# An fp32r transformer block on one Trainium2 core: activation tiles moved to other places of 512 bytes

## What is computed

```python
# first block: mixer, then gated FFN
y = sigmoid(ga) * ((hm * gain * sigmoid(om)) @ w_mlstm_down) + sigmoid(gb) * y_b
mix = y @ w_mix_out
f = (gelu(causal_dwconv(gate)) * val) @ w_ffn_down      # val, gate = split(h @ w_ffn_up)
# second block: attention and conformer convolution, cross attention, MLP
xq = rmsnorm(h, norm_x_g) @ w_xq
mn = rmsnorm(mem, norm_mem_g);  xk = mn @ w_xk;  xv = mn @ w_xv
h = h + xo @ w_xo
h = h + square(relu(rmsnorm(h, norm_mlp_g) @ w_up)) @ w_down
```

## Time and profile before

| | us |
|---|---|
| median of 2 runs | 1605.63 |
| the runs | 1605.50, 1605.77 |
| span of the profiled execution | 1604.7 |
| TensorE busy in the span | 1574.8 |
| weight loads | 1289.5 |
| VectorE busy | 753.8 |
| ScalarE busy | 637.3 |
| GpSimd busy | 680.4 |

### The profile page before, as it was taken

One profiled execution on the slowest core, in us unless ns is written; L12 is line 12 of the kernel. 1 busy time (PEld: TensorE's weight loads), 2 busy tenths in 40 slices (PEclk: granted clock), 3 DMA queues, 4 the chain that ended last, 5 costly groups with the idle time before them and its releaser, 6 DMA issues.

```text
span 1604.7 us, 19156 instructions
## 1 busy us (share of the span) xinstructions
PE 1574.8 (98%) x7560; PEld 1289.5 (80%) x7560; DVE 753.8 (47%) x1333; ACT 637.3 (40%) x1145; POOL 680.4 (42%) x518
## 2 busy tenths in 40 slices
PE   7999999999997999999999999999999999999998
PEld 5788867788896888888888887778878888888886
DVE  5999424646586352133308799752442421012203
ACT  3543563453434332233322335672452442224322
POOL 1584233244543544444455464004314444444442
PEclk8999999999999999999999999999999999999999
DMA  9576522278533353333333432002212332333332
GB/s 316 131 114 148 132 79 79 65 224 289 196 92 118 107 171 124 98 101 92 97 123 102 137 105 89 5 14 79 80 39 84 102 103 99 99 93 92 105 94 78
DMA packets 221706, 180.31 MB, mean 112 GB/s; under 512 B 24232, under 2 KB 184360, under 8 KB 221488
## 3 DMA queue, kind: packets, MB, share of 16 engines
q1 hardware_dynamic: 214512, 167.00, 35.8%
q10 hardware_dynamic: 7104, 12.08, 2.2%
HBM read 172.49 MB, written 6.55 MB: 112 GB/s over the span
## 4 chain that ended last, share of the span: by engine, by line
PE 76%; DVE 4%; ACT 2%; POOL 0%; issue 0%; DMA 0%; DVEq 0%; ACTq 0%
PE bank L631 13%; PE bank L632 13%; PE bank L637 13%; PE bank L714 9%; PE bank L713 9%; PE bank L718 9%; PE bank L758 2%; PE bank L1105 1%; PE bank L1076 1%; PE bank L741 1%; PE bank L742 1%; PE bank L743 1%; PE bank L1162 1%; PE bank L967 1%; PE bank L1148 0%; PE bank L1149 0%
## 5 line engine op out<-in xcount | busy, mean ns | idle before, releaser
L2455 POOL TENSOR_TENSOR w_lo<-raw,w_hi 128x512 fp32r<-128x512 f32 (+1 forms) x484 | 646.6, 1360 | 871.6 <-ACT w_hi L1232 871.0
L1232 ACT ACTIVATE w_hi<-raw 128x512 fp32r<-128x512 f32 (+1 forms) x484 | 276.2, 620 | 336.5 <-PE bank L718 255.9
L631 PE MATMUL bank<-h_hi,w_hi 128*128 128x512 f32 x936 | 367.2, 392 | 0.0
L632 PE MATMUL bank<-h_lo,w_hi 128*128 128x512 f32 x936 | 364.3, 389 | 0.0
L637 PE MATMUL bank<-h_hi,w_lo 128*128 128x512 f32 x936 | 250.3, 389 | 0.0
L631 PEld LDWEIGHTS bank<-h_hi,w_hi 128*128 128x128 f32 x936 | 175.7, 188 | 39.0 <-issue 2.4
L632 PEld LDWEIGHTS bank<-h_lo,w_hi 128*128 128x128 f32 x936 | 175.7, 188 | 36.6 <-issue 0.7
L637 PEld LDWEIGHTS bank<-h_hi,w_lo 128*128 128x128 f32 x936 | 175.7, 188 | 36.6
L2282 DVE SCALAR_TENSOR_TENSOR bank<-att_area,cols,bank 128x512 f32<-128x512 f32 x116 | 87.6, 755 | 3.9
L713 PE MATMUL bank<-w_hi,u_hi 128*128 128x512 f32 x224 | 87.1, 389 | 0.0
L714 PE MATMUL bank<-w_hi,u_lo 128*128 128x512 f32 x224 | 87.1, 389 | 0.0
(11 more groups left out here) (439 smaller groups left out, 2639.9 us busy)
## 6 DMA issues: line engine op xcount, KB each, us to landing
raw<-in_w_in SPq DMA_DIRECT2D x57, 512.0 KB, 4.2
raw<-in_w_ffn_up SPq DMA_DIRECT2D x44, 512.0 KB, 3.9
raw<-in_w_up SPq DMA_DIRECT2D x32, 512.0 KB, 4.0
raw<-in_w_down SPq DMA_DIRECT2D x32, 512.0 KB, 3.7
ada_ring<-in_w_ada SPq DMA_DIRECT2D x24, 512.0 KB, 5.8
raw<-in_w_ffn_down SPq DMA_DIRECT2D x20, 512.0 KB, 3.7
raw<-in_w_s_glu SPq DMA_DIRECT2D x16, 256.0 KB, 3.1
raw<-in_w_mlstm_down SPq DMA_DIRECT2D x8, 512.0 KB, 6.7
```

The source lines that it names most:

```text
L631: te.matmul(ps, wv[0][:, i, :], rh, start=(i == 0), stop=False)
L632: te.matmul(ps, wv[0][:, i, :], rl, start=False, stop=False)
L1232: sc.activation(W_HI[SLOT[key]][:, part_], raw[:, RAW_SLOT[key], part_], ACT.Copy).then_inc(*hi_set.up((key, n_)))
L2455: gp_.tensor_tensor(W_LO[s_][:, part_], raw[:, RAW_SLOT[key], part_], W_HI[s_][:, part_].bitcast(F32), ALU.subtract).then_inc(*lo_made.up( ...
```

## The change

Only places of tiles in SBUF. The assertion asks for even elements instead of multiples of 128. No instruction is added, removed or reordered.

```diff
--- before.py
+++ after.py
@@ -186,7 +186,7 @@
             for s_ in shape:
                 n *= s_
             assert BASE + 4 * (at + n) <= END, name
-            assert dt == F32 or at % P == 0, name
+            assert dt == F32 or at % 2 == 0, name
             return nc.alloc_sbuf_tensor_at(name, [P, *shape], dt, offset=BASE + 4 * at)
 
         NRAW, NSPL, BW, NSCR = 3, 3, 1024, 3
@@ -267,7 +267,7 @@
         y_hi = place("y_hi", X + 8192, [KD, S], F32R)
         y_lo = place("y_lo", X + 12288, [KD, S], F32R)
         g_hi = place("g_hi", X + 4096, [KD, S], F32R)
-        g_lo = place("g_lo", X + 23680, [KD, S], F32R)
+        g_lo = place("g_lo", X + 23680 + 48, [KD, S], F32R)
         flat_branch = branch[:, :, :].rearrange("p a b -> p (a b)")
         xn2 = flat_branch.rearrange("p (t d) -> p t d", t=TT)
 
@@ -275,20 +275,20 @@
 
         tail_m = place("tail_m", X + 4096, [4, BW], F32R)
         tail_f = place("tail_f", X + 16384, [4, BW], F32R)
-        tail_u = place("tail_u", X + 18432, [4, BW], F32R)
+        tail_u = place("tail_u", X + 18432 + 128, [4, BW], F32R)
         tail_h = place("tail_h", 4096, [8, BW], F32R)
         TAILS = [(buf, i) for buf, n in ((tail_m, 2), (tail_f, 2), (tail_u, 2), (tail_h, 4)) for i in range(n)]
         W_HI = [w_hi[:, i, :] for i in range(NSPL)] + [buf[:, 2 * i, :] for buf, i in TAILS]
         W_LO = [w_lo[:, i, :] for i in range(NSPL)] + [buf[:, 2 * i + 1, :] for buf, i in TAILS]
 
         xkT = place("xkT", X + 25728, [KD, NMEM])
-        mn_hi = place("mn_hi", X + 23680, [KD, NMEM], F32R)
-        mn_lo = place("mn_lo", X + 21632, [KD, NMEM], F32R)
+        mn_hi = place("mn_hi", X + 23680 - 8, [KD, NMEM], F32R)
+        mn_lo = place("mn_lo", X + 21632 - 8, [KD, NMEM], F32R)
         mem_tok = part(flat_branch, 0, MT, D)
 
         xv = place("xv", X, [MT, D])
-        act_hi = place("act_hi", X + 2048, [FH, S], F32R)
-        act_lo = place("act_lo", X + 7680, [FH, S], F32R)
+        act_hi = place("act_hi", X + 2048 - 64, [FH, S], F32R)
+        act_lo = place("act_lo", X + 7680 - 32, [FH, S], F32R)
         rows_f = place("rows_f", X + 13312, [3 * D])
         tmp_f = place("tmp_f", X + 16384, [TT * D])
         cv_t = place("cv_t", X + 20480, [2, S])
@@ -311,20 +311,20 @@
         c_tok = part(aa, 14848, TT, DA)
 
 
-        x_hi = place("x_hi", X + 6144, [KD, S], F32R)
-        x_lo = place("x_lo", X + 10240, [KD, S], F32R)
+        x_hi = place("x_hi", X + 6144 + 16, [KD, S], F32R)
+        x_lo = place("x_lo", X + 10240 + 48, [KD, S], F32R)
         xqT = place("xqT", X + 2048, [KD, S])
         xps_t = place("xps", X + 17408, [XH, TT, NMEM])
         xps = [xps_t[:, h] for h in range(XH)]
         xpT_t = place("xpT", X + 21504, [2, MT, S])
         xpT = [xpT_t[:, i] for i in range(2)]
-        xo_hi = place("xo_hi", X + 9216, [KD, S], F32R)
-        xo_lo = place("xo_lo", X + 13312, [KD, S], F32R)
-
-        u_hi = place("u_hi", X, [UH, S], F32R)
-        u_lo = place("u_lo", X + 8192, [UH, S], F32R)
-        rel = place("rel", X + 16384, [4, S])
-        squares = place("squares", X + 22528, [2 * TT, S])
+        xo_hi = place("xo_hi", X + 9216 - 32, [KD, S], F32R)
+        xo_lo = place("xo_lo", X + 13312 - 16, [KD, S], F32R)
+
+        u_hi = place("u_hi", X + 16, [UH, S], F32R)
+        u_lo = place("u_lo", X + 8192 + 112, [UH, S], F32R)
+        rel = place("rel", X + 16384 + 128, [4, S])
+        squares = place("squares", X + 22528 + 128, [2 * TT, S])
 
         def col(name, i=0, n=1, p0=0, p1=P):
             at = COL_AT[name] + i
```

## The result

The changed kernel takes 1613.42 us (median of 2 runs, 1612.86 and 1613.99) against 1605.63: a ratio of 1.0058, 95% interval 1.0038 to 1.0078. It is slower by half a per cent, which is small but clear of the uncertainty. The forecast was no effect.

What follows compares the result with a forecast made beforehand. The prediction took TensorE's matmul count times pitch to bound the kernel. Steps 1 and 2 added 0 + 0 to the 1604.7 us span, so it forecast the earlier median, 1605.6 us, with a range of 1583 to 1633 us.

Steps and rivals of the forecast that it cites:

- What bounds the kernel: Whole kernel: TensorE, busy 98% of 1604.7 us, so time is the number of matmuls times their pitch.
- Step 1: Matmuls reading moved tiles, 2032 in all: start places leave the pitch unchanged, 0 us, bounds -22.4 to +27.0 us.
- The term I set at 0: Change in the fixed extra per fp32r matmul that reads a moved tile, claimed 0 on 2032 matmuls.
- The bounds it took from rows: On 2032 matmuls: extra falls to 2.5 ns, -22.4 us; or a second 13.3 ns is added, +27.0 us.
- Step 2: ScalarE and VectorE writing the moved tiles: slower writes stay covered, 0 us, bounds 0 and +0.3 us.
- the faster one: Fp32r matmuls: the fixed 11 ns are a collision at the common start; up to 22.4 us saved, 1583.2 us; chance 0.17.
- The slower one: Fp32r matmuls: common start is harmless, other starts add a mid-load meeting, 13.3 ns each, +27.0 us, 1632.6 us; chance 0.24.
- The mixed one: Moved tiles: some places help, others hurt, sum within 10 us of no change; chance 0.07.

Runs made afterwards that it cites:

- 1064: Kernel of fp32r matmuls alone, 48 in a row: moving slice 64 bytes behind the weights' place, against distance 0 at 226.7 ns; settles at 228.8 ns per matmul.
- 3064: Same kernel of matmuls alone, with moving slice and weights both moved 64 bytes, against both at the common place: 10.92 us for 48, 226.7 ns once settled.

## Why the prediction was wrong

What bounds the kernel: right. The time followed the pitch of the fp32r matmuls alone.

Step 1, the matmuls: this is the step that failed, in its argument about the distance between the two reads: it "grows by about 480 bytes during one load: nearly one whole turn of 512", so that "a collision that depends on the distance modulo 512, or on a fraction of it, then happens as often from any start, and the sum is unchanged". It supposes that each meeting costs the same and leaves the rhythm alone. For a 128-column load the pitch should then be the same from any start, and the runs show 226.7 to 236.7 ns. They show a price that isn't a sum of meetings: a 32-column load costs 5 ns more than a 128-column one at distance 0, one distance holds three pitches by what went before, and a distance of 64 bytes gives 228.8 ns where 208 gives 234.6. The period is 256 bytes. The term I set at 0 measured +4.5 ns on u's 768, +4.3 on act's 528, +6 to 7 on xo and mn in xv, +3.5 on x, +4.4 on g's 192, and -1.7 on mn's 192 of 256 columns.

The count of step 1 was short as well: "of g only the 64 that read g_lo". All 192 matmuls of g slowed, so 2160 matmuls changed their pitch and not 2032, and the 128 that read the unmoved g_hi carry between 0.5 and 0.6 of the 8.7 us.

The value was chosen because it was "nearest to the f32 rows with unequal places". Those rows were read rightly and say nothing of fp32r: plain f32 is at 429.2 ns at all eight distances. The text said that they stream at half the rate and don't settle fp32r, and then let them settle it. The bounds it took from rows, -22.4 and +27.0 us, held the result.

By the Trainium skill ("TensorE: Matmul & The Clock Gate", what happens when you issue a matmul) loading the next weights doesn't take read bandwidth from the running matmul. The Trainium skill ("SBUF — State Buffer", who interferes with whom), on which the prediction leaned, gives PE two independent read ports and has it wait on nobody. By that no placement should matter. These runs differ, and the measurement decides: with the moving slice 64 bytes on, the pitch settles at 228.8 ns while the weights are at the common place (1064), and at 226.7 ns when they are 64 bytes on too (3064). Whether the two reads wait on each other is not shown.

Step 2, the writers: right. u_hi went from 634 to 632 ns and u_lo from 722 to 723.

The rivals: the faster one is out for 512 columns, where nothing over all distances is below 226.7 ns. The slower one had the sign, and a price of 13.3 ns that was three times too large; its mechanism, one more meeting in mid-load, isn't shown and shares the fault of step 1. The mixed one comes nearest, with 7.7 us, one gain and six losses; it had a chance of 0.07, for which the prediction gives no reason.

What stays open: why 226.7 ns (512 / 2.4 + 13.3) is the rhythm that streams lock into, what has a period of 256 bytes, and how the places of the matmuls before act on later ones. The runs tell on which distances the pitch hangs, not by what mechanism.

## What to carry to other kernels

With weight loads of 128 columns, put fp32r weights and all activations at the same place modulo 256 bytes: then every matmul of 512 columns runs at the best pitch seen, and 8 bytes or more away from it they may lose 1 to 4%. One tile out of place slows its neighbours too, so move all or none. Where a trace shows one case only, all operands equally placed here, it can't price another; matmuls alone, one line of code per setting, do it in one run. An operation at half the rate is no stand-in for the full rate.

## What was not expected of the hardware

- The fp32r pitch at 512 columns depends on the distance of the two operands modulo 256 bytes: 226.7 ns at 0, 228.8 at 64, 231 to 237 at nearly all others, by steps of 16 bytes; plain f32 is at 429.2 at the eight distances tried.
- The pitch has memory. At a distance of 240 bytes the stream kept 226.7, 233.3 or 236.7 ns to the end of its 48 matmuls, by what ran before it. In the network 64 matmuls with all operands at the common place ran at 232.0 ns beside others that weren't, and at 226.7 without them.
- A weight load of 32 columns can cost more than one of 128: 231.7 against 226.7 ns at distance 0.
- At 256 columns the common place is not the best: 120.0 against 117.7 ns.
